# Sigmoid of the all-keys heads' gates by Exp, Ln and Exp in place of Tanh

## The reference

```python
px = split_cols(hx @ w_in)
ya, yca = global_gqa(...)          # 8 heads, all latent and context keys, rmsnorm on q and k, rope
yb, ycb = neighbourhood_attn(...)  # 8 heads
yc_, ycc = window_gqa(...)         # 8 heads, rope
ux = jnp.concatenate([ya, yb, yc_], axis=-1) * jax.nn.silu(px[9])
x = x + gate[:, None, :] * (ux @ w_out)
```

## Time and profile before

| | us |
|---|---|
| median of 3 runs | 2935.71 |
| lowest and highest | 2934.6 and 2936.95 |
| the profiled execution, its own time | 2937.72 |
| its span, first to last instruction | 2935.8 |
| PE busy in the span | 2817.1 |
| DVE busy | 1359.6 |
| ACT busy | 770.6 |
| mean granted clock of TensorE | 0.991 |

### The profile page before, as it was taken

The page is one execution under the profiler, slowest core; times in us unless marked ns, Lnnn a source line. Parts: engine busy times, 40 slices in busy tenths (PEclk is TensorE's granted clock), DMA queues, the critical chain, the costliest instruction groups (busy, mean ns, idle before and its releaser), DMA issues.

```text
span 2935.8 us, 33844 instructions
## 1 busy us (share of the span) xinstructions
PE 2817.1 (96%) x13312; PEld 1524.2 (52%) x13312; DVE 1359.6 (46%) x2569; ACT 770.6 (26%) x1410; POOL 224.9 (8%) x253
## 2 busy tenths in 40 slices
PE   7999999999999999999999989999999999999998
PEld 3656555655555556576444644444445735444442
DVE  2687675885355664774575741111115813121112
ACT  3333554440223452423251120000003231000001
POOL 2324112100011000000000000000002300000000
PEclk9999999999999999999999999999999999999999
DMA  8235211132244321231210158999993217999996
GB/s 312 88 131 183 68 59 51 65 144 72 92 148 167 122 87 44 87 124 68 72 58 15 66 207 365 421 422 421 421 420 144 103 66 303 411 421 421 421 420 282
DMA packets 90672, 586.59 MB, mean 200 GB/s; under 512 B 10192, under 2 KB 10192, under 8 KB 29232
## 3 DMA queue, kind: packets, MB, share of 16 engines
q1 hardware_dynamic: 69696, 502.56, 42.7%
q0 software_dynamic: 20848, 82.26, 8.2%
HBM read 582.68 MB, written 2.10 MB: 199 GB/s over the span
## 4 chain that ended last, share of the span: by engine, by line
PE 68%; DVE 7%; ACT 2%; issue 1%; DVEq 0%; ACTq 0%
PE BIG L1129 43%; PE PJ L1129 11%; PE BIG L1973 4%; PE PT L1458 2%; PE PT L1474 2%; DVE ARENA L3016 1%; PE PT L1129 1%; PE BIG L1441 1%; PE PJ L1178 1%; PE BIG L1445 1%; PE PT L1949 1%; DVE ARENA L3068 0%; ACT ARENA L2177 0%; DVE ARENA L3067 0%; PE BIG L1434 0%
## 5 line engine op out<-in xcount | busy, mean ns | idle before, releaser
L1129 PE MATMUL BIG<-ARENA 128*64 128x512 f32 (+3 forms) x2720 | 566.1, 458 | 6.5 <-DVE ARENA L3090 2.5
L1129 PEld LDWEIGHTS BIG<-ARENA 128*64 128x64 f32 (+1 forms) x2720 | 303.1, 169 | 255.2 <-issue 224.1
L1129 PE MATMUL PJ<-HT,W 128*128 128x512 f32 (+2 forms) x1040 | 398.1, 531 | 7.4 <-DVE ARENA L2726 2.6
L1129 PE MATMUL BIG<-W,ARENA 128*64 128x512 f32 (+1 forms) x1280 | 282.0, 573 | 0.9 <-DVE ARENA L2938 0.9
L1129 PEld LDWEIGHTS PJ<-HT,W 128*128 128x128 f32 x1040 | 192.6, 192 | 165.2 <-issue 125.6
L3119 DVE SCALAR_TENSOR_TENSOR XC<-BIG,MOD,XC 128x512 f32<-128x512 f32 x128 | 90.2, 747 | 379.7 <-PE BIG L1973 379.7
L2188 ACT ACTIVATE ARENA<-PT 128x512 f32<-128x512 f32 (+1 forms) x264 | 145.2, 583 | 408.5 <-PE PT L1458 408.2
L1129 PE MATMUL BIG<-HT,W 128*128 128x512 f32 (+1 forms) x600 | 237.5, 554 | 2.4 <-DVE ARENA L2892 2.1
L1129 PEld LDWEIGHTS BIG<-W,ARENA 128*64 128x64 f32 (+1 forms) x1280 | 107.4, 142 | 161.0 <-issue 154.9
L2755 DVE TENSOR_REDUCE STAT<-BIG 128x1 f32<-128x512 f32 (+5 forms) x240 | 169.8, 724 | 40.4 <-PE BIG L1445 35.5
L1129 PE MATMUL BIG<-HT,ARENA 128*64 128x512 f32 (+1 forms) x632 | 182.9, 573 | 0.0
(11 more groups left out here) (325 smaller groups left out, 2998.8 us busy)
## 6 DMA issues: line engine op xcount, KB each, us to landing
ARENA<-in_exp_w SPq DMA_DIRECT2D x168, 1024.0 KB, 18.1
W<-in_exp_w SPq DMA_DIRECT2D x144, 1024.0 KB, 16.8
W<-in_units SPq DMA_DIRECT2D x89, 1024.0 KB, 4.9
HT<-in_exp_w SPq DMA_DIRECT2D x72, 1024.0 KB, 22.0
W<-in_mod_rows POOLq DMA_DIRECT2D x67, 512.0 KB, 3.9
ARENA<-in_mod_rows POOLq DMA_DIRECT2D x61, 512.0 KB, 4.1
ARENA<-in_bias_b POOLq DMA_DIRECT2D x16, 384.0 KB, 5.8
XC<-in_x SPq DMA_DIRECT2D x1, 3072.0 KB, 11.1
```

The costliest lines, as they stand in the source:

```text
L1129: ins = pe.matmul(out, lhsT, rhs, start=start, stop=stop, skip_group_check=skip)
```

## The change

For pairs of kind A, Tanh is replaced by three activations, in both layers, each waiting for the one before. The constants that DVE adds and multiplies follow (0.0 for 1.0, 1.0 for 0.5); a third column of `EPSC` holds the 1.0 that Ln adds. The explicit preload of the Tanh set after layer 1's q norm is gone, and `square` preloads the set with Ln and Exp only for the keys, that is once per layer, at A0.

```diff
+            def sigmoid_by_logarithm(dst, src):
+                act.activation(dst, src, ACT.Exp, scale=-1.0).then_inc(act_chain, 1)
+                act.wait_ge(act_chain, me.next("act_chain"))
+                act.activation(dst, dst, ACT.Ln, bias=EPSC[:, 2:3]).then_inc(act_chain, 1)
+                act.wait_ge(act_chain, me.next("act_chain"))
+                act.activation(dst, dst, ACT.Exp, scale=-1.0).then_inc(gate_tanh, 1)
...
-                            act.activation(GATE_T[:, a:b], src, ACT.Tanh, scale=0.5).then_inc(gate_tanh, 1)
+                            if kind == "A":
+                                sigmoid_by_logarithm(GATE_T[:, a:b], src)
+                            else:
+                                act.activation(GATE_T[:, a:b], src, ACT.Tanh, scale=0.5).then_inc(gate_tanh, 1)
...
-                        act.activation(GATE_T, SG[:, x % 2, :], ACT.Tanh, scale=0.5).then_inc(gate_tanh, 1)
+                        if PAIRS[x][0] == "A":
+                            sigmoid_by_logarithm(GATE_T, SG[:, x % 2, :])
+                        else:
+                            act.activation(GATE_T, SG[:, x % 2, :], ACT.Tanh, scale=0.5).then_inc(gate_tanh, 1)
...
-                        if what == "norm_q" and layer:
-                            act.preload_act_table(ACT.Tanh)
...
-            def square(raw):
+            def square(raw, first=False):
...
-                act.preload_act_table_set("natural_log_exp_and_others")
+                if first:
+                    act.preload_act_table_set("natural_log_exp_and_others")
...
-                            dve.scalar_tensor_tensor(SG[:, i % 2, a:b], GATE_T[:, a:b], 1.0,
+                            more = 0.0 if PAIRS[i][0] == "A" else 1.0
+                            dve.scalar_tensor_tensor(SG[:, i % 2, a:b], GATE_T[:, a:b], more,
...
+            dve.memset(EPSC[:, 2:3], 1.0)
```

More of the change, by code:

```diff
@@ L488, in build @@
         COEF = sb("COEF", [P, 16])
-        EPSC = sb("EPSC", [P, 2])
+        EPSC = sb("EPSC", [P, 3])
         STAT = sb("STAT", [P, 12])
@@ L2095, in attention @@
                             else:
-                                square((use, dst, n))
+                                square((use, dst, n), which == "k")
                     elif what == "block":
@@ L2128, in attention @@
                             act.wait_ge(qk_normed, me.seen["qk_normed"])
-                        square((raw_use[which, i], K[:, kv % 2, :] if which == "k" else Q[:, i % 2, :], NA))
+                        square((raw_use[which, i], K[:, kv % 2, :] if which == "k" else Q[:, i % 2, :], NA),
+                               which == "k")
                     elif what == "tanh":
@@ L2595, in attention @@
                         dve.wait_ge(gate_tanh, me.next("gate_tanh"))
-                        dve.scalar_tensor_tensor(SG[:, x % 2, :], GATE_T, 1.0, SG[:, x % 2, :],
-                                                 ALU.add, ALU.mult).then_inc(gated, 1)
+                        dve.scalar_tensor_tensor(SG[:, x % 2, :], GATE_T, 0.0 if PAIRS[x][0] == "A" else 1.0,
+                                                 SG[:, x % 2, :], ALU.add, ALU.mult).then_inc(gated, 1)
                         dve.wait_ge(gated, me.next("gated"))
@@ L2644, in attention @@
                         y = query_tile(i, t, U[:, i, :])
-                        dve.scalar_tensor_tensor(y, like_query_tile(i, t, PT[:, bank:bank + P]), 0.5,
+                        dve.scalar_tensor_tensor(y, like_query_tile(i, t, PT[:, bank:bank + P]),
+                                                       1.0 if PAIRS[i][0] == "A" else 0.5,
                                                  query_tile(i, t, SG[:, i % 2, :]), ALU.mult, ALU.mult)\
```

## The result

The changed kernel takes 2956.51 us (median of 6 runs, 2953.74 to 2957.05); the kernel before, on the same chip, 2935.04 (6 runs, 2933.18 to 2936.95). The ratio is 1.0069, with a 95% interval of 1.0060 to 1.0079: **slower by 21.5 us**. The forecast was 13.7 slower (2949.4), with a range of 2941 to 2957; the time lies in it, close to its upper end.

The account below looks back on a forecast made before the run. PE, busy 96% of the span, was taken to bound the kernel, so added ACT time costs only where PE waits. Chains of 10.3 and clock falls of 3.4 made 13.7 us more, 2949.4, range 2941 to 2957.

Parts of the forecast that it names:

- A1 to A3 in layer 0: Queries' norm: two new loads delay PE's rope, less 1.28 gained at the copies; 1.08 us per pair, 3.2 for three.
- A0 in layer 0: Queries' norm: two new loads, 2.57 us, less 0.4 from an earlier bank copy, all reaching PE; 2.2 us.
- Gates in layer 0: Three activations and two loads make ACT 3.0 us later, mostly covered by its idle time; costed at nothing.
- Gates in layer 1: Bare chain of three activations ahead of DVE's rope: 1.41 us more at A0, 1.17 each at A1 to A3.
- The sum of the chains: Norms and gates of both layers, as delays reaching PE without the clock: 3.2 + 2.2 + 1.4 + 3.5 = 10.3 us.
- Loads: 16 table loads of 1.28 us in layer 0's pairs; loads removed in layer 1 gain nothing, C0's new one costs 0.
- The clock: Granted clock may fall behind new waits at A0 in layer 0 and A0 to A3 in layer 1; two falls, 3.4 us.
- the clock falls in all five places: Rival: a clock fall at A0 in layer 0 and A0 to A3 in layer 1 costs 8.5; 2954.5 us, chance 0.20 less: 0.12.
- The clock holds: Rival: no clock fall behind the new waits, only the exposed chains cost; 2946.0 us, chance 0.20.
- layer 0 comes out even: Rival: the copies' gain and idle time cover layer 0's loads, only layer 1's 4.9 stay; 2940.6 us, chance 0.08.
- the shared set: Rival: no table switch between Ln and Exp in layer 0's four pairs, so no change; 2936.8 us, chance 0.06.

Follow-up runs that it names:

- one_set: The changed kernel, but layer 0's second vectors step preloads the set with Ln and Exp instead of Tanh's: 2941.22 us, ratio 1.0017 to the kernel before.
- layer0_only: The changed kernel with layer 1's heads as before (Tanh and both preloads back), layer 0's as changed: 2944.88 us, ratio 1.0032 to the kernel before.
- layer1_only: The changed kernel with layer 0's heads as before (Tanh, preload after each square), layer 1's as changed: 2947.38 us, ratio 1.0037 to the kernel before.
- fill_waits: The changed kernel with unread matmuls in PE's eight waits, four in layer 0 and five in layer 1 each: 2954.38 us, ratio 1.0060 to the kernel before.
- fill_less: The changed kernel with unread matmuls in PE's eight waits, two in layer 0 and three in layer 1 each: 2945.46 us, ratio 1.0027 to the kernel before.
- one_set_rope_first: one_set with DVE making the queries' rope of A0 to A3 in layer 1 ahead of the gates' product: 2926.41 us, ratio 0.9966 to the kernel before.

## Why the prediction was nearly right, and which term was mis-sized

- **What bounds.** PE's waits behind ACT and DVE were the right question; freed ACT time bought nothing: behind the loads taken away in layer 1, no wait of PE changed.
- **A1 to A3 in layer 0.** Forecast 1.08 each. PE stopped waiting 1.28 for the copies and waits 2.18 for the rope, "about 2.2" in the prediction. As waits that is 0.90 each, 2.7 in all against 3.2. The mechanism stood, a gain and a later loss on one engine.
- **A0 in layer 0.** Forecast 2.2: 1.75 and 0.35 more, 2.1, in two pieces on either side of the queries' rope, as said.
- **Gates in layer 0**, costed at nothing: in the changed kernel PE has no new wait behind them, and at 419.30 ACT is still idle 0.94 ahead of the copy of PE's next transposes; `one_set` has the three activations without their loads and no new wait either.
- **Gates in layer 1.** Forecast waits of 2.90 at A0 and 2.95 at the others; the rows have 2.91 and 2.95. The Ln's price was off by 0.002.
- **The sum of the chains.** Forecast 10.3; 9.8 by the rows, 9.7 measured with the clock held (5.3 to 10.6 by the interval).
- **Loads.** 16 in layer 0's pairs at 1.28 each, and C0's ended 7.11 before Tanh had its input, so it costs nothing. The drain of the Trainium skill ("ScalarE: Activation LUTs", What ACT_TABLE_LOAD costs) doesn't show after the change either: in layer 0 the load at 405.58 takes 1.28 and Ln starts at 406.88, 0.02 later.
- **The clock: the step that failed.** The prediction named five places and took two falls at 1.7 each, 3.4. There were seven falls, worth up to 15.3, or 9.9 with two old falls and 2.0 of a wait gone, and some 11 by the run with the waits filled. Two things were wrong in that step. The list of places left out A1 to A3 in layer 0, though the text itself gave them new waits of 2.2, near the 2.56 after which the clock had fallen; all three fell. Of the five on the list four fell, all but A0 in layer 1. And each fall was priced at the 3.4 us of one row; two of the seven lasted 6.8, as one of before's own had (1559.9 to 1566.7). The counter-example, 2.70 of idle PE without a fall, was given too much weight. That a later wait would shrink and an old fall go with it (A0, layer 0) wasn't foreseen either; it worked the other way. Why some places keep the clock isn't settled.
- **Luck.** The time lies within the range by 0.5 us. The exposed chains and the seven falls without what came back are 2935.7 + 9.8 + 15.3 = 2960.8, past the upper end; what brought it in, the two old falls and the shorter wait, was not in the prediction.

The rival "the clock falls in all five places" (2954.5) came nearest in time, 2.0 off where the forecast was 7.1 off; its mechanism is the one that was seen, but with one of its places wrong and three missing. "The clock holds" is refuted by the windows, "layer 0 comes out even" by `layer0_only`, and the shared set by the 16 loads. Where the set is shared, in `one_set`, the time isn't that rival's 2936.8 either but 5.3 over before, with falls of the clock at all four pairs of layer 1.

## What to carry to other kernels

Where a change adds waits to a busy TensorE, list every place, and price a fall of the clock at each beside the wait: here new waits of 1.75 to 2.95 brought seven falls in eight places, which cost about as much as the waits (some 11 beside some 9.7). Before a formula is blamed, look at which table set is active where it runs and at what stands behind its result in the next engine's order: one preload by name and one product moved behind the rope turned 21.5 us slower into 9.3 faster. A fill has to be sized from a measured row, since one of 4.56 in a wait of 2.9 gives back what it gains.

## What the runs showed of the hardware

- The granted clock stood at 0.50 after waits of PE of 2.18 in layer 0, three times out of three in the changed kernel, and again with layer 0 alone. At A0 in layer 1 PE waited 2.91 in the changed kernel, in `layer1_only` and in `one_set` alike; the clock stayed at 1.00 in the first and fell in the other two. Ahead of C0 in layer 1 PE waited 2.55 or 2.56 in all nine traces, and the clock fell in five (before, `layer0_only`, `fill_waits`, `fill_less`, `one_set_rope_first`) and stayed in four. The length of the last wait alone doesn't decide it.
- In these places, stretches at the lower level lasted 3.4 or 6.8 us, so a fall costs up to 1.7 or 3.4: PE was busy for 5.96 to 6.03 of the long ones and 3.37 to 3.40 of the short ones in the changed kernel.
- A table load that the build puts ahead of an activation need not wait for that activation's input: C0's load began at 1179.42, 8.4 us ahead of its Tanh at 1187.82, which started when PE's product was there.
